# Triangular inverse of the delta rule: the packed even columns of both token blocks turned by one full transpose per head

## The reference, cut to what matters

```python
a_low = jnp.where(strict, jnp.einsum('bhnid,bhnjd->bhnij', k_beta, k) * decay, 0.0)
t_inv = lax.linalg.triangular_solve(eye + a_low, jnp.broadcast_to(eye, a_low.shape),
                                    left_side=True, lower=True, unit_diagonal=True)
u = t_inv @ (v * beta[..., None])
w = t_inv @ (k_beta * jnp.exp(gc)[..., None])
```

## Time and profile before

| what | value |
|---|---|
| median of three timed executions | 1568.95 us (1568.45 to 1569.41) |
| profiled execution: first to last instruction (span) | 1563.7 us |
| median less span | 5.2 us |
| PE busy | 1521.7 us, 97% of the span |
| DVE, ACT, POOL busy | 36%, 24%, 12% |
| DMA in the last 24 of 40 slices | busy share 9 tenths or more in 22 of them |
| granted TensorE clock, mean | 0.997 of full speed |

### The profile page before, as it was taken

How to read it: one execution, slowest core, us unless ns; L and a number is a source line. 1 busy time by engine, 2 the same in 40 slices (tenths; PEclk the granted TensorE clock), 3 DMA queues, 4 the chain that set the end, 5 groups by cost and what they waited for, 6 DMA issues and landing times.

```text
span 1563.7 us, 34934 instructions
## 1 busy us (share of the span) xinstructions
PE 1521.7 (97%) x15639; PEld 1043.7 (67%) x15639; DVE 558.4 (36%) x803; ACT 379.3 (24%) x604; POOL 184.3 (12%) x182
## 2 busy tenths in 40 slices
PE   9999999999999998999999999999999999999997
PEld 7778888777777787733756765666657557556544
DVE  5754455585857666421212121121212112121113
ACT  5554344564645463210000000000000000000000
POOL 0100000134433325100000000000000000000100
PEclk9999999999999999999999999999999999999999
DMA  9237555542232300699999999999999999999991
GB/s 350 95 129 229 189 186 188 188 154 90 82 109 76 114 1 2 276 415 408 409 410 408 405 409 407 406 411 405 406 408 411 404 407 411 405 408 408 412 410 80
DMA packets 145354, 450.38 MB, mean 288 GB/s; under 512 B 10624, under 2 KB 41888, under 8 KB 130880
## 3 DMA queue, kind: packets, MB, share of 16 engines
q1 hardware_dynamic: 141680, 437.10, 72.5%
q0 software_dynamic: 3536, 11.14, 1.8%
HBM read 440.87 MB, written 7.34 MB: 287 GB/s over the span
## 4 chain that ended last, share of the span: by engine, by line
PE 87%; DVE 9%; ACT 1%; issue 1%; DMA 1%; POOL 1%; SPq 0%; POOLq 0%; DVEq 0%; ACTq 0%
PE banks L1980 37%; PE banks L1997 19%; PE banks L1470 8%; PE banks L1472 7%; PE banks L1471 7%; DVE cvall L1157 2%; DVE wlo L959 2%; PE banks L1899 1%; PE banks L1889 1%; PE banks L1880 1%; DMA raw<-in_attn_w_qkv_dram 1%; DVE T L1217 1%; PE banks L1937 1%; PE banks L1599 1%; PE banks L1908 0%
## 5 line engine op out<-in xcount | busy, mean ns | idle before, releaser
L1980 PE MATMUL banks<-ring,xg 128*32 128x512 f32 (+1 forms) x6144 | 585.0, 539 | 0.0
L1980 PEld LDWEIGHTS banks<-ring,xg 128*32 128x32 f32 x6144 | 288.2, 110 | 278.7 <-issue 267.9
L1292 DVE TENSOR_TENSOR ehid<-banks,esil 64x768 f32<-64x768 f32 (+1 forms) x64 | 89.4, 1396 | 722.6 <-ACT esil L888 722.2
L1997 PE MATMUL banks<-ring,ehT 128*32 128x256 f32 x5376 | 304.0, 379 | 1.2
L1997 PEld LDWEIGHTS banks<-ring,ehT 128*32 128x32 f32 x5376 | 231.8, 110 | 70.8 <-issue 17.6
L888 ACT ACTIVATE esil<-banks 64x1536 f32<-64x1536 f32 (+1 forms) x32 | 41.0, 1283 | 784.2 <-PE banks L1980 784.2
L959 DVE TENSOR_TENSOR wlo<-raw,whi 128x2048 fp32r<-128x2048 f32 x74 | 179.8, 2431 | 79.7 <-ACT whi L638 79.6
L1470 PE MATMUL banks<-whi,xhi 128*128 128x512 f32 x448 | 182.5, 407 | 5.8 <-DVE X L1143 2.8
L1472 PE MATMUL banks<-whi,xlo 128*128 128x512 f32 x448 | 175.2, 391 | 0.0
L1471 PE MATMUL banks<-wlo,xhi 128*128 128x512 f32 x448 | 174.9, 390 | 0.0
L638 ACT CAST whi<-raw 128x2048 fp32r<-128x2048 f32 x74 | 141.1, 1906 | 48.9 <-PE banks L1472 44.3
(11 more groups left out here) (312 smaller groups left out, 1255.5 us busy)
## 6 DMA issues: line engine op xcount, KB each, us to landing
ring<-in_moe_w_gate_dram SPq DMA_DIRECT2D x112, 1024.0 KB, 11.3
ring<-in_moe_w_up_dram SPq DMA_DIRECT2D x112, 1024.0 KB, 12.7
ring<-in_moe_w_down_dram SPq DMA_DIRECT2D x112, 1024.0 KB, 12.0
raw<-in_dn_w_in_dram SPq DMA_DIRECT2D x16, 1024.0 KB, 5.2
raw<-in_ffn_w_gate_dram SPq DMA_DIRECT2D x22, 512.0 KB, 4.1
raw<-in_ffn_w_up_dram SPq DMA_DIRECT2D x22, 512.0 KB, 5.0
raw<-in_ffn_w_down_dram SPq DMA_DIRECT2D x11, 1024.0 KB, 4.9
raw<-in_dn_w_in_dram SPq DMA_DIRECT2D x16, 512.0 KB, 4.5
```

Source lines behind the costliest of these rows:

```text
L1292: i = dve.tensor_tensor(ehid[64 * s:64 * s + 64, 0:TILES * n_ // 2].rearrange("p (t k j) -> p t k j", t=TILES, k=k_), by_row(src, s), by_r ...
L1980: last = pe.matmul(bank[first_bank + t][TILE * q:TILE * (q + 1), 0:n_].rearrange("p (s c) -> p s c", s=2), xg[:, t, kt, :], w[q // 2][:, k ...
L1997: i = pe.matmul(token_tile(3, t, q, 256), eT[:, h_:h_ + TILE], w[:, at_:at_ + 256], start=first and m == 0 and k == 0 and t % 2 == 0, stop ...
```

## The change

Three edits:
- The layout of `Ec` goes from number 4*block + head to head-major, so that the 64 packed columns of block 0 and block 1 of one head lie side by side, 128 in all.
- ACT packs `Ec` in all six levels; level 6 did without before. Per group these are four more copies of 128x128 (L850).
- T becomes one 128x128 transpose per head: four transposes a level in place of eight f32 products. The partitions and columns of the result are the same, so all that reads it is unchanged. The wait for `Ec_ready` now stands in level 6 too.

```diff
-    Ec = at("Ec", 8 * 64, W0 + 10)[:, :].rearrange("p (n f) -> p n f", n=8)
+    Ec = at("Ec", 8 * 64, W0 + 10)[:, :].rearrange("p (h b f) -> p h b f", h=GH, b=TB)
...
-                    if lv < LEVELS - 1:
-                        for q in range(2):
-                            act.wait_ge(*((sem("TT_ready"), 4 * (u - 1) + 2 * q + 2) if lv > 1 else (sem("TT0_ready"), 2 * g + 2)))
-                            for b in range(TB):
-                                n_ = slice(4 * b + 2 * q, 4 * b + 2 * q + 2)
-                                i = act.copy(of_blocks(Ec[:, n_, :], lv, None), of_blocks(TT[:, n_, :], lv, 0))
-                            i.then_inc(sem("Ec_ready"), 1)
+                    for q in range(2):
+                        act.wait_ge(*((sem("TT_ready"), 4 * (u - 1) + 2 * q + 2) if lv > 1 else (sem("TT0_ready"), 2 * g + 2)))
+                        for b in range(TB):
+                            n_ = slice(4 * b + 2 * q, 4 * b + 2 * q + 2)
+                            i = act.copy(of_blocks(Ec[:, 2 * q:2 * q + 2, b, :], lv, None), of_blocks(TT[:, n_, :], lv, 0))
+                        i.then_inc(sem("Ec_ready"), 1)
...
-                        if lv < LEVELS - 1:
-                            pe.wait_ge(sem("Ec_ready"), 2 * (g * (LEVELS - 2) + lv - 1) + q + 1)
+                        pe.wait_ge(sem("Ec_ready"), 2 * u + q + 1)
                         for h in (2 * q, 2 * q + 1):
-                            for b in range(TB):
-                                i = pe.matmul(bank[q][64 * b:64 * b + 64, h % 2 * P:(h % 2 + 1) * P],
-                                              (Ec if lv < LEVELS - 1 else TT)[:, 4 * b + h, 0:64], ident, start=True, stop=True)
+                            i = pe.transpose(bank[q][:, h % 2 * P:(h % 2 + 1) * P], Ec[:, h].rearrange("p b f -> p (b f)"), ident)
```

## The result

Twenty executions of the changed kernel took 1570.62 to 1574.24 us, median 1572.59; twenty of the kernel before, on the same chips, 1567.23 to 1570.90, median 1569.39. The ratio is 1.0023 (95% interval 1.0017 to 1.0028): the change makes the kernel slower by 3.2 to 3.6 us, where a gain of 5.3 was forecast.

The account below looks back on a forecast made before the run. The experts were taken as paced by a weight transfer that cannot start before `o_done`. Gains of 4.95 + 0.15 + 0.2 = 5.3 us off 1568.95 gave 1563.65, stated as 1563.6; own range 1562.5 to 1565.4, 8-in-10 range 1562.2 to 1566.4.

Parts of the forecast that it names:

- T from 0.88 to 0.44 us, and the switch of array mode that only changes place: Each level's T: 0.44 us saved, the 0.19 us half-to-full-array switch moving ahead of T; 0.45 taken, ends 0.38 and 0.49.
- Ten filled levels of groups 1 and 2: Levels 2 to 6 of groups 1 and 2, with filling work and room in their waits, each gain 0.45 us.
- Group 0: Level 2 gains 0.45 us, levels 3 and 4 together 0.15, unfilled levels 5 and 6 0.03 each.
- `Tc` hardly moves: Group 0, level 3: ACT's cast behind `Tc` stays near 369.57, so the `wlo` starts only 0.15 us earlier.
- First levels pass nothing on: Level 1 of each group: dT's weight load waits for `Pc` behind a 3.2 us `wlo`; gain taken as 0.
- Unfilled levels, 0.03 each: Levels 5 and 6 of group 0, 2 to 6 of group 3: 0.03 us gained each, 0.2 over seven.
- Level 6's `Ec` copies cost nothing: Level 6, each group: four new `Ec` copies are covered, cost 0; if uncovered, 1.9 us over four groups.
- From `o_done` on one for one: Behind the last group's output: any time gained at `o_done` reaches the end in full, with nothing between touched.
- The sum: Whole kernel: 4.95 + 0.15 + 0.2 = 5.3 us gained, bounds 3.6 to 6.4.
- The clock falls in the last group: Rival, group 3: thinner PE work drops the clock to half, 12 us more, time 1575.7 us; chance 0.07.
- the row held against the rival: Group 3, 601.6 to 604.7 us: PE busy only 1.56 of 3.10 us, yet clock 1.00; cited against a clock fall.

Follow-up runs that it names:

- e5: Changed kernel with the old products back in level 1 of group 3 only; ratio to the kernel before 0.9943, median 1561.45 us.
- e8: Changed kernel plus five unread 128x512 products in level 1 of group 3 only; ratio to the kernel before 0.9954, median 1563.68 us.
- e9: Changed kernel with DVE's last `wlo` moved from level 1 of group 3 to behind the group; ratio to the kernel before 0.9953, median 1562.15 us.
- e1: Changed kernel with the old products back in all of group 3; ratio to the kernel before 0.9964, median 1560.82 us.
- e4: Changed kernel plus unread 128x512 products in group 3, five in level 1, one in each later level; ratio to the kernel before 0.9959, median 1559.39 us.
- e2: Changed kernel with products back in groups 0 to 2, transposes in group 3 only; ratio to the kernel before 1.0055, median 1575.10 us.
- e7: Changed kernel with one pair of heads back to products in every level of group 3; ratio to the kernel before 1.0030, median 1575.11 us.
- e6: Changed kernel with products back in levels 2 to 6 of group 3, transposes in level 1; ratio to the kernel before 0.9950, median 1563.31 us.
- e3: Changed kernel with each transpose in group 3 issued twice; ratio to the kernel before 0.9971, median 1561.74 us.

## Why the prediction was wrong, step by step

- **T from 0.88 to 0.44 us, and the switch of array mode that only changes place**: right. T and the first product behind it went from 1.31 to 0.82 us, 0.49 for 0.45 taken; the upper end of its bounds. The first transpose starts 0.15 us behind the last product of P and the second 0.17 behind the first, then 0.11 apart, in the trace of group 1.
- **Ten filled levels of groups 1 and 2**: right, 2.38 and 2.41 us for 2.25 each.
- **Group 0**: 1.06 us, for 0.45 + 0.15 + 0.06. Levels 3 and 4, taken at 0.15 together, gave 0.42: level 3 gave 0.48 and level 4 took 0.06 back. The wrong reading here is "`Tc` hardly moves". The two `Tc` copies ended 0.37 us earlier, so the cast was done at 369.23 and not at 369.57, at the same time as `TT`, and the `wlo` began at 369.26, half a microsecond earlier than before. It then took 2.44 us for 2.29.
- **First levels pass nothing on**: right, dT's load still waits for `Pc` in group 3.
- **Unfilled levels, 0.03 each**: at full clock 0.08 (group 3 in e5, e8 and e9: 15.32 us for 15.72, five levels). The first `Tc` copy starts 0.40 us behind the end of P (e9), where it started 0.49 behind it before; the prediction had 0.41 for 0.44. This term was under-sized; it is small.
- **Level 6's `Ec` copies cost nothing**: right. No wait for `Ec` shows in the profile after, and L1886 is followed by L1469 or dT as in other levels.
- **From `o_done` on one for one**: right in the main. On one chip (e1 to e4) L437 came between 629.23 and 643.59 us, and the time from the first expert product to the end stayed at 895.6 to 896.1. But "nothing between the two" is untouched only up to the 1.6 us of luck behind L437 told above.
- **The sum**: at full clock the four differences are 1.06 + 2.38 + 2.41 + 0.40 = 6.3 us, for 5.3. So the terms of the gain were sound; the sum left out a term.
- **The step that failed is the choice among the rivals.** The sum put the clock in group 3 at nothing: every term is priced at full clock. "The clock falls in the last group" had a chance of 0.07 and a price of 12 us. It is what happened, in the profile and, by their times and mean clocks (0.985 to 0.988), in all twenty executions. Its price was 22.09 - 15.32 = 6.8 us between dT of level 1 and dT of level 6, for which 6 x 0.8 = 5 was reckoned, and 3.6 behind them, for 7: the clock returned at 629.55, before `o_done`. In all 10.3 us, against a gain of 6.3. The price came near by two errors that offset each other in part. PE's share of the chain was put at 1.2 us a level, but before show 0.68 + 0.90 + 0.88 and e5 0.68 + 0.90 + 0.38 = 1.96; and half clock was taken to last up to `o_done`, where it ended 6 us behind the levels.
- **What misled**: the row held against the rival, PE busy 1.56 of 3.10 us at clock 1.00, was the very stretch where it then fell. It showed that this stretch held, not by how much. The comparison to be made was the stretch after the edit, with T cut from 16 records to four: in level 1 of group 3 only P and T of PE stand between `TT` and `Pc`. The same stretch in the profile after, with the same columns:

```profile
596.11:599.20 3.09, 1.28 (x20) 1.00 (x20) 3.09 (x3) 1.39 (x6) 3.09 (x2) 0.94 0.00 0
```

1.28 us of work in place of 1.56, and the clock fell 0.4 us before dT. The change took away the work where it was scarcest; e1 shows that even with the products the clock can fall there for 3.4 us. The second half of the mechanism, that a thin stretch which would hold the clock does not win it back, had no row in the trace of before; it was priced as half clock up to `o_done` without a reason for its length.

## What to carry to other kernels

Before shortening TensorE's work, find the stretches where it is already the thinnest, and take the granted clock there as a thing that the change can lose: here a cut that gained 6 us at full clock cost 10 by the clock of one thin stretch. Guard or leave out those stretches; here mending a single level, or moving one DVE instruction that made PE wait there, turned +3.6 us into -7 to -9. And a stretch that keeps a full clock is no proof that it would regain a lost one.

## What the runs showed of the hardware

- A low clock persists in work that does not lose it: with transposes in levels 2 to 6 it stayed at 0.50 for 27.3 to 30.7 us once lost (after, e2; e7 with half of the transposes) and did not fall in the profiles where level 1 was mended (e5, e8, e9). With products there it was back after 3.4 and 6.8 us (e1, e6).
- Transposes, eight a level, held the clock as products do (e3, in ten executions).
- Behind the DeltaNet the clock falls in every profile, for 3.4 us in eight of them and 6.8 in six, and the longer fall costs 1.6 us.
- From full-array work to half-column tiles and back the price is met once for each change, not for each block: 0.19 us behind half-column products, none behind transposes. In a filled level, moving a block across this border cost nothing in sum (0.59 + 0.23 us for T and the product behind it, where 0.44 + 0.24 + 0.19 was to be expected from the rows of before).
- The profile's span and its execution differ by 1.8 us; medians of before ran from 1566.7 to 1569.8 us between chips, as much as the effect in question.
